# Scan stage of a Mamba-2 layer: operands loaded for four chunks at once, gates by chunk, output weights behind

## The reference

```python
def step(state, inp):
    x, dtq, bq, cq = inp
    cs = jnp.cumsum(dtq * a_g, axis=1)
    seg = cs[:, :, None] - cs[:, None, :]
    decay = jnp.exp(jnp.where(causal[None, :, :, None, None], seg, -jnp.inf))
    xdt = x * dtq[..., None]
    cb = jnp.einsum('bign,bjgn->bijg', cq, bq)
    y = jnp.einsum('bijgh,bjghp->bighp', cb[..., None] * decay, xdt)
    y = y + jnp.einsum('bign,bghpn->bighp', cq, state) * jnp.exp(cs)[..., None]
    to_end = jnp.exp(cs[:, -1:] - cs)
    state = state * jnp.exp(cs[:, -1])[..., None, None] + jnp.einsum(
        'bjgn,bjghp->bghpn', bq, to_end[..., None] * xdt)
    return state, y
# afterwards: y + d_skip * x, times silu(z), a grouped RMSNorm, the output projection
```

## Time and profile before

| | us |
|---|---|
| median of 3 runs (lowest to highest) | 3037.1 (3032.89 to 3038.3) |
| the profiled execution, its own time | 3036.6 |
| its span, first to last instruction | 3034.8 |
| TensorE / VectorE / ScalarE / GpSimd busy in the span | 2692.9 / 1908.8 / 1553.8 / 641.3 |
| scan stage, 1812 to 2117 us: TensorE / VectorE / ScalarE / GpSimd busy | 198.9 / 181.0 / 78.5 / 144.8 of 305 |
| mean granted TensorE clock in that stage, DMA share, GB/s | 0.80, 0.67, 165 |

### The profile page before, as it was taken

One profiled execution on the slowest core, in us unless ns is written; L12 is line 12 of the kernel. 1 busy time (PEld: TensorE's weight loads), 2 busy tenths in 40 slices (PEclk: granted clock), 3 DMA queues, 4 the chain that ended last, 5 costly groups with the idle time before them and its releaser, 6 DMA issues. The chain is left out here.

```text
span 3034.8 us, 40407 instructions
## 1 busy us (share of the span) xinstructions
PE 2692.9 (89%) x13762; PEld 2157.4 (71%) x13762; DVE 1908.8 (63%) x2393; ACT 1553.8 (51%) x1794; POOL 641.3 (21%) x530
## 2 busy tenths in 40 slices
PE   7998999987999999939999986676998799999992
PEld 6885677756887777828888864555787588888772
DVE  5335766337888888855235315665543688888885
ACT  4234555226888888744223212222122488888883
POOL 0000000003343343420000004544000134443340
PEclk9998999998999999959999997887999899999996
DMA  4325110146999999843223226665212599999995
GB/s 145 89 47 155 36 43 22 49 155 252 374 371 371 372 370 371 305 154 100 80 90 121 84 85 171 163 164 144 107 42 98 203 387 383 374 372 371 367 361 203
DMA packets 347895, 618.71 MB, mean 204 GB/s; under 512 B 33320, under 2 KB 135232, under 8 KB 347648
## 3 DMA queue, kind: packets, MB, share of 16 engines
q1 hardware_dynamic: 322880, 570.94, 55.3%
q0 software_dynamic: 19136, 33.61, 3.0%
q10 hardware_dynamic: 5760, 12.59, 1.1%
HBM read 566.55 MB, written 86.13 MB: 215 GB/s over the span
## 5 line engine op out<-in xcount | busy, mean ns | idle before, releaser
L2334 DVE TENSOR_TENSOR moe_w_low<-moes_raw,moe_w_high 128x2048 fp32r<-128x2048 f32 x384 | 868.5, 2289 | 163.3 <-ACT moe_w_high L2263 162.6
L2263 ACT ACTIVATE moe_w_high<-moes_raw 128x2048 fp32r<-128x2048 f32 x384 | 725.3, 1917 | 125.5 <-PEq L150 56.7
L2130 POOL COPY moe_pick<-moes_tokens 128x1 int32 (+1 forms) x64 | 88.6, 1384 | 595.2 <-PE moe_px L2179 594.5
L174 PE MATMUL moe_py<-moe_w_high,moe_h_high 128*128 128x512 f32 x512 | 209.1, 408 | 0.0
L174 PE MATMUL moe_pg<-moe_w_high,moe_x_high 128*128 128x512 f32 x512 | 205.1, 401 | 3.6 <-DVE moe_x_low L2384 3.6
L174 PE MATMUL moe_pu<-moe_w_high,moe_x_high 128*128 128x512 f32 x512 | 204.3, 399 | 0.0
L176 PE MATMUL moe_pg<-moe_w_high,moe_x_low 128*128 128x512 f32 x512 | 201.1, 393 | 0.0
L176 PE MATMUL moe_py<-moe_w_high,moe_h_low 128*128 128x512 f32 x512 | 201.0, 393 | 0.0
L176 PE MATMUL moe_pu<-moe_w_high,moe_x_low 128*128 128x512 f32 x512 | 200.6, 392 | 0.0
L175 PE MATMUL moe_pg<-moe_w_low,moe_x_high 128*128 128x512 f32 x512 | 200.0, 391 | 0.0
L175 PE MATMUL moe_py<-moe_w_low,moe_h_high 128*128 128x512 f32 x512 | 199.7, 390 | 0.0
(11 more groups left out here) (386 smaller groups left out, 6356.8 us busy)
## 6 DMA issues: line engine op xcount, KB each, us to landing
moes_raw<-in_w_gate SPq DMA_DIRECT2D x128, 1024.0 KB, 12.4
moes_raw<-in_w_up SPq DMA_DIRECT2D x128, 1024.0 KB, 12.6
moes_raw<-in_w_down SPq DMA_DIRECT2D x128, 1024.0 KB, 12.4
sproj_raw<-in_w_in_ssd SPq DMA_DIRECT2D x40, 512.0 KB, 4.2
comb_rows<-Y SPq DMA_DIRECT2D x32, 512.0 KB, 8.7
scan_sums<-CSR SPq DMA_DIRECT2D x32, 512.0 KB, 9.6
XC<-sproj_c SPq DMA_DIRECT2D x24, 512.0 KB, 5.0
HN<-plan_hn SPq DMA_DIRECT2D x16, 512.0 KB, 3.0
```

The costliest lines, as they stand in the source:

```text
L174: nc.tensor.matmul(out, lh, rh, start=start, stop=False)
L2130: nc.gpsimd.tensor_copy(pick[a][:, :], M.tokens[:, bass.ds(b, 1)]).then_inc(picked[a], 1)
L2263: nc.scalar.activation(wh[c % SPLIT_SLOTS][:, :], M.raw[j][:, :], ACT.Copy).then_inc(w_high, 1)
L2334: nc.vector.tensor_tensor(wl[j][:, :], M.raw[c % RAW_SLOTS][:, :], bits(wh[j][:, :]), ALU.subtract).then_inc(w_low, 1)
```

## The change

`LOAD = 4` chunks are loaded together. `bT`, `cT`, `xT` and `sums` get buffers four chunks wide, two of each instead of four narrow ones; `z` and `y` keep their ring of four. SyncE's new `operands(q)` loads quad q (half a group's chunks): two DMAs of 256 KB, one of 1024 KB and one of 2048 KB for sums. `gates(n)` loads z of one item. The semaphores are split: `loaded` (bT, cT, xT; TensorE waits for it), `sums_loaded` (VectorE) and `z_loaded` (GpSimd). From quad 2 on, `operands(q)` waits for `y_done` and, ahead of sums, for `seg_ok` of the last item of quad q - 2, but in SyncE's order it stands behind `gates(4q - 1)`, which waits until item 4q - 5 is gated. SyncE begins with quad 0, the z of items 0 to 3, quad 1, and then `early_dma`. No compute operation is added or removed; their operands are slices of the wide buffers.

```diff
--- before.py
+++ after.py
@@ -1384,13 +1384,13 @@
 
     GW, KT = HG * HD, HG * HD // P
     ITEMS = [(g, c) for g in range(G) for c in range(NT)]
-    NI, RING = len(ITEMS), 4
+    NI, RING, LOAD = len(ITEMS), 4, 4
     with Stage(nc, "scan") as st:
         PAR = range(2)
-        xT = [st.sb(f"xT{a}", [P, KT, P]) for a in range(RING)]
-        bT, cT = ([st.sb(f"{n}{a}", [P, P]) for a in range(RING)] for n in ("bT", "cT"))
+        xT = [st.sb(f"xT{a}", [P, KT, LOAD * P]) for a in PAR]
+        bT, cT = ([st.sb(f"{n}{a}", [P, LOAD * P]) for a in PAR] for n in ("bT", "cT"))
         z, y = ([st.sb(f"{n}{a}", [P, GW]) for a in range(RING)] for n in "zy")
-        sums = [st.sb(f"sums{a}", [P, HG, P]) for a in range(RING)]
+        sums = [st.sb(f"sums{a}", [P, HG, LOAD * P]) for a in PAR]
         cbm = [st.sb(f"cbm{a}", [P, P]) for a in PAR]
         dec, W = ([st.sb(f"{n}{a}", [P, HG, P]) for a in PAR] for n in ("dec", "W"))
         bt = [st.sb(f"bt{a}", [P, N]) for a in PAR]
@@ -1399,7 +1399,8 @@
         state = st.sb("state", [P, GW])
         pcb, pbt, pyi, pst = (st.ps(n, [P, HALF]) for n in ("pcb", "pbt", "pyi", "pst"))
         px, py = ([st.ps(f"{n}{a}", [P, GW]) for a in PAR] for n in ("px", "py"))
-        loaded, y_stored = ([st.sem(f"{n}{a}") for a in range(RING)] for n in ("loaded", "y_stored"))
+        z_loaded, y_stored = ([st.sem(f"{n}{a}") for a in range(RING)] for n in ("z_loaded", "y_stored"))
+        loaded, sums_loaded = ([st.sem(f"{n}{a}") for a in PAR] for n in ("loaded", "sums_loaded"))
         cb_done, x_turned, yi_done, st_done, y_done = (st.sem(n) for n in ("cb_done", "x_turned", "yi_done", "st_done", "y_done"))
         bt_ok, xs_ok, e_ok, ss_ok = (st.sem(n) for n in ("bt_ready", "xs_ready", "decay_ready", "squares"))
         cbm_ok, seg_ok, xdt_ok, yi_ok, y_ok, st_ok = (st.sem(n) for n in ("cbm_ready", "seg_ready", "xdt_ready", "yi_ready", "y_ready", "state_ready"))
@@ -1424,47 +1425,67 @@
         def byhead(x):
             return x.rearrange("p (h d) -> p h d", h=HG)
 
+        def chunk(n):
+
+            return n // LOAD % 2, slice(n % LOAD * P, (n % LOAD + 1) * P)
+
         def arrived(eng, n):
-            eng.wait_ge(loaded[n % RING], (n // RING + 1) * 80)
+            eng.wait_ge(loaded[n // LOAD % 2], (n // (2 * LOAD) + 1) * 48)
 
         @block.sync
         def _(sp):
-            early_dma(sp)
-            for n, (g, c) in enumerate(ITEMS):
-                a, tok = n % RING, slice(c * P, (c + 1) * P)
-                if n >= RING:
-                    sp.wait_ge(y_done, n - RING + 1)
-                    sp.wait_ge(gated, n - RING + 1)
-                    sp.wait_ge(seg_ok, n - RING + 1)
+            def operands(q):
+                (g, c), a = ITEMS[q * LOAD], q % 2
+                tok = slice(c * P, (c + LOAD) * P)
+                if q >= 2:
+                    sp.wait_ge(y_done, (q - 1) * LOAD)
                 for buf, first in ((bT, DI // P), (cT, DI // P + G)):
                     sp.dma_start(buf[a][:, :], K.XC[g + first, :, tok]).then_inc(loaded[a], 16)
                 sp.dma_start(xT[a][:, :, :], K.XC[g * KT:(g + 1) * KT, :, tok].rearrange("k p n -> p k n")).then_inc(loaded[a], 16)
-                sp.dma_start(sums[a][:, :, :], K.CSR[g * HG:(g + 1) * HG, tok].partition_broadcast(P)).then_inc(loaded[a], 16)
-                sp.dma_start(z[a][:, :], K.Z[tok, g * GW:(g + 1) * GW]).then_inc(loaded[a], 16)
+                if q >= 2:
+                    sp.wait_ge(seg_ok, (q - 1) * LOAD)
+                sp.dma_start(sums[a][:, :, :], K.CSR[g * HG:(g + 1) * HG, tok].partition_broadcast(P)).then_inc(sums_loaded[a], 16)
+
+            def gates(n):
+                (g, c), a = ITEMS[n], n % RING
+                if n >= RING:
+                    sp.wait_ge(gated, n - RING + 1)
+                sp.dma_start(z[a][:, :], K.Z[c * P:(c + 1) * P, g * GW:(g + 1) * GW]).then_inc(z_loaded[a], 16)
+
+            operands(0)
+            for n in range(RING):
+                gates(n)
+            operands(1)
+            early_dma(sp)
+            for n in range(RING, NI):
+                if n % LOAD == 0 and n >= 2 * LOAD:
+                    operands(n // LOAD)
+                gates(n)
 
         @block.tensor
         def _(pe):
             def front(n):
-                r = n % RING
+                r, tok = chunk(n)
                 arrived(pe, n)
                 if n:
                     pe.wait_ge(cbm_ok, n)
-                nc.tensor.matmul(pcb[:, 0:P], bT[r][:, :], cT[r][:, :], start=True, stop=True).then_inc(cb_done, 1)
+                nc.tensor.matmul(pcb[:, 0:P], bT[r][:, tok], cT[r][:, tok], start=True, stop=True).then_inc(cb_done, 1)
                 if n >= 2:
                     pe.wait_ge(xs_ok, n - 1)
                 if n:
                     pe.wait_ge(bt_ok, n)
                 for k in range(KT):
-                    nc.tensor.transpose(px[n % 2][:, k * P:(k + 1) * P], xT[r][:, k, :], K.ident)
-                nc.tensor.transpose(pbt[:, 0:P], bT[r][:, :], K.ident).then_inc(x_turned, 1)
+                    nc.tensor.transpose(px[n % 2][:, k * P:(k + 1) * P], xT[r][:, k, tok], K.ident)
+                nc.tensor.transpose(pbt[:, 0:P], bT[r][:, tok], K.ident).then_inc(x_turned, 1)
 
             def back(n):
-                (g, c), a, r = ITEMS[n], n % 2, n % RING
+                (g, c), a = ITEMS[n], n % 2
+                r, tok = chunk(n)
                 if c:
                     pe.wait_ge(st_ok, states(n - 1))
                     if from_state(n) > 1:
                         pe.wait_ge(yi_ok, from_state(n) - 1)
-                    nc.tensor.matmul(pyi[:, :], cT[r][:, :], state[:, :], start=True, stop=True).then_inc(yi_done, 1)
+                    nc.tensor.matmul(pyi[:, :], cT[r][:, tok], state[:, :], start=True, stop=True).then_inc(yi_done, 1)
                 if c + 1 < NT:
                     pe.wait_ge(bt_ok, n + 1)
                     pe.wait_ge(xde_ok, states(n))
@@ -1480,7 +1501,7 @@
                         pe.wait_ge(w_lo, n + 1)
                     if k == KT // 2:
                         pe.wait_ge(w_hi, n + 1)
-                    nc.tensor.matmul(py[a][:, k * P:(k + 1) * P], xT[r][:, k, :], skip[g % 2][:, k, :, :], start=True, stop=False)
+                    nc.tensor.matmul(py[a][:, k * P:(k + 1) * P], xT[r][:, k, tok], skip[g % 2][:, k, :, :], start=True, stop=False)
                     for h in (2 * k, 2 * k + 1):
                         last = nc.tensor.matmul(py[a][:, h * HD:(h + 1) * HD], W[a][:, h, :], xdt[a][:, h * HD:(h + 1) * HD],
                                                 start=False, stop=(h % 2 == 1))
@@ -1526,14 +1547,15 @@
             V = nc.vector
 
             def front(n):
-                (g, c), a, r = ITEMS[n], n % 2, n % RING
-                arrived(dve, n)
+                (g, c), a = ITEMS[n], n % 2
+                r, tok = chunk(n)
+                dve.wait_ge(sums_loaded[r], (n // (2 * LOAD) + 1) * 16)
                 if n >= 2:
                     dve.wait_ge(w_lo, n - 1)
                     dve.wait_ge(w_hi, n - 1)
                 for h in range(HG):
                     own = K.heads[:, CS, c, g * HG + h:g * HG + h + 1]
-                    last = V.tensor_scalar(dec[a][:, h, :], sums[r][:, h, :], own, 0.0, ALU.subtract, ALU.min)
+                    last = V.tensor_scalar(dec[a][:, h, :], sums[r][:, h, tok], own, 0.0, ALU.subtract, ALU.min)
                 last.then_inc(seg_ok, 1)
                 dve.wait_ge(cb_done, n + 1)
                 V.tensor_tensor(cbm[a][:, :], pcb[:, 0:P], K.upper, ALU.mult).then_inc(cbm_ok, 1)
@@ -1599,7 +1621,7 @@
             def gate(n):
                 a, r = n % 2, n % RING
                 pool.wait_ge(y_ok, n + 1)
-                arrived(pool, n)
+                pool.wait_ge(z_loaded[r], (n // RING + 1) * 16)
                 if n >= RING:
                     pool.wait_ge(y_stored[r], n // RING * 16)
                     pool.wait_ge(ss_ok, n - RING + 1)
```

## The result

The changed kernel takes 2982.8 us (median of four runs, 2980.02 to 2986.79) against 3037.7 us for the one before in the same comparison: a ratio of 0.982, with a 95% interval of 0.9804 to 0.984. That is 55 us less. The forecast was 2983.

What follows compares the result with a forecast made beforehand. It took VectorE's stalls on scan loads, mostly sums, as the bound. Loop saving 55.7 us plus 3.6 at the start minus 6 for late quads, 53.3 off 3036.6, gave 2983 us; range 2957 to 3033.

Steps and rivals of the forecast that it cites:

- What bounds the kernel before: Scan stage: VectorE loses 34 us in the loop to load stalls; sums is more than half of each load's time.
- (a): Scan loads: a quad's sums in 2 KB runs takes 10.5 us, interpolated towards the final gain's 4 KB row.
- (b): Scan start: with w_out moved behind the first loads, VectorE starts at 1829.5 instead of 1833.10, 3.6 us earlier.
- (c): Steady state of the scan loop: sums about half a microsecond late, charged 1 us on each of six quads, 6 us.
- A + 22.5: Time item 8's front wants its sums, counted from A, the start of item 3's y addition; sums predicted at A + 23.0.
- (d): Scan loop on VectorE: 31 periods of 7.1 us plus ends, 226.7 us against 282.4, saving 55.7 us.
- The cover: Scan loop: TensorE needs only 5.3 us an item at its upper clock level, which was expected to hold.
- Rival 1: Scan sums: repeated reads stay as slow per byte, 22 to 26 us a quad; 3061 to 3089 us, chance 0.11.
- Rival 2: Scan sums: no penalty at 2 KB, no late quads; 2972.5 us, or 2959 with periods of 6.66; chance 0.16.
- Rival 3: Scan loop: TensorE falls to 1.2 GHz in part, or its waits fill in; period 8.0 us, 3011 us, chance 0.18.
- Rival 4: Scan loop: stalls were only cover, VectorE's waits before y additions grow; 3031 to 3043 us, chance 0.05.
- The rule on 512 B: Scan sums: 512 B is the least transfer for line rate, so wider packets would bring sums nothing.

Runs made afterwards that it cites:

- e9: Changed kernel with bT, cT, xT and sums each loaded in four one-chunk DMAs of 512 B runs: 3035.0 us.
- e1: Changed kernel with the output weights (w_out, 4 MB) issued ahead of the first quad, as before: 2994.0 us.
- e3: Changed kernel with only bT, cT and xT in 512 B runs, sums staying in 2 KB runs: 2988.3 us.
- e11: Changed kernel with only sums in 512 B runs, read from eight different blocks with a row per partition, so decays are wrong: 3015.1 us.
- e2: Changed kernel with only sums in four DMAs of 512 B runs, the other operands staying in 2 KB runs: 3022.2 us.
- e12: Changed kernel with GpSimd's fade of the state cut from 512 to 64 columns, leaving seven of eight heads' states unfaded: 2966.2 us.
- e8: Changed kernel with scan_dec moved from VectorE to ScalarE, the sign turned round in the exponential: 2961.9 us.
- e10: e8 with GpSimd making xde ahead of its upper half of W: 2941.8 us.

## Why the prediction was right, point by point

The time was right, to less than a microsecond, and that closeness is luck. The mechanism was right, but its terms were not as good as the total: two were off by about 6 us each in opposite directions, and a third by 2.4.

- **What bounds the kernel before.** Right. The stalls came from the loads, sums took most of each load, and the wait's removal left VectorE as the bound. e9 shows that nothing is left of the gain without the long runs; e1, that some 11 of the 55 us need the output weights behind as well.
- **(a) Sums of a quad, 10.5 us.** Wrong in size: 6.2 us, 338 GB/s. The step that failed is the interpolation "three sevenths of the way" between 86 to 101 ns for a packet at 512 B and 262 ns at 4 KB. There is no such slope from 512 B on: a single load's packet has 88 to 102 ns at 512 B, 1 KB and 2 KB. The straight line put 161 to 170 ns where 97 were measured. At 2 KB this is near the rate of ordinary loads (370 GB/s, 89 ns a packet), so the bound from the full rate (5.7 us) was the one to take. Why the 4 KB row moved more slowly than that, at 205 to 300 GB/s, no run shows; it was a load of 512 KB, a quarter of the size. "The run length matters only for a repeated source" was right (e3 and e11).
- **(b) The start, 3.6 us earlier.** 6.0 were measured. 2.4 us more: sums landed 6.1 us behind xT instead of 11.1, and xT at 8.3 us after the stage's start (issued 0.8 in, landing 7.5 later) instead of 5.8. The 0.6 us for completion stands in no row.
- **(c) 6 us for late quads.** None came late: VectorE waits for sums once. With sums at 6.2 instead of 10.5 us a quad lands about 4 us before it is wanted, by the prediction's own account (A + 18.7 against A + 22.5). z for the gates and the queued 4 MB cost nothing, as said.
- **(d) The loop, 226.7 us.** 233.1 were measured. The cover held: the granted clock is 0.94 in the mean from 1824 to 2056 us (lower for short stretches, as 0.50 from 1874 to 1876, in which VectorE is busy throughout), and one y addition waits for scan_py. The mis-sized term is the period: 7.3, not 7.1. It was taken from dense items that came singly or in pairs, where the engines had just come out of a stall or went into one, and the longest was of two items. In an unbroken run two or more GpSimd operations stand beside nearly every group (26 of 30): 3.65 us in the mean, up to 5.07.
- **The sum.** The 4.3 us too much for sums made the 6 of (c), and in (b) with the late xT against it 2.4; (d) was 6.4 too little. The stage came out at 247.6 us against 16.9 + 232.7 = 249.6 predicted.
- **Rival 1** fell: a repeated read is not the same bytes per second at 2 KB. e9 and e2 show what it would have cost here: not 3061 to 3089, but 3022 to 3035. The stalls are 5 to 7 us, not 12 to 16, since four short-run loads in the queue take about 16 us and not 22 to 26. **Rival 2** had the packets right, and named 2972.5; it was off by the period. **Rival 3** fell by its cause (the clock is 1.00 from 1900 to 1932 us, 0.91 over the stage, and VectorE hardly waits), though its effect, a longer period, came in small and by way of GpSimd. **Rival 4** fell with the waits.
- **The rule on 512 B** (the Trainium skill, DMA: Bandwidth & Descriptors, section Specifications). By it e2 should have been as fast as the changed kernel. It is 39 us slower, and e11, with the same packets from a source that isn't repeated, has the changed kernel's loop. The measurement decides: here the rule holds for ordinary rows and not for rows that all partitions read.

## What to carry to other kernels

A load that spreads few rows over all partitions is worth longer runs: for the same 2.10 MB, 2 KB runs were some 2.6 times as fast here as 512 B runs. Runs beyond 2 KB were not tried. Ordinary loads can stay as they are. When stalls go, a period read from single dense items is a lower bound (7.1 against 7.3 here, and the longest stretch, of two items, would have given no more): count what the neighbouring engine will have beside them in an unbroken run. Where VectorE is the bound, an operation shortened on GpSimd can bring nearly as much (16.6 us, e12) as work taken from VectorE itself (21 us, e8); and once that is done, the order on GpSimd can be what TensorE waits for (20 us, e10).

## What the runs showed of the hardware

- A single load of 1024 packets from a source that all 128 partitions read takes 6.5, 5.6 and 6.2 us at 512 B, 1 KB and 2 KB a packet: 81, 187 and 338 GB/s. Four loads of 512 B packets queued together take 15.0 to 17.9 us (e2), 117 to 140 GB/s. The same 512 B packets from different rows moved at 291 to 302 GB/s (e11).
- A GpSimd operation of 1.04 to 1.3 us costs VectorE 0.8 to 1.0 us when it falls on scan_dec or scan_W, and is often longer itself, 1.50 or 1.64 instead of 1.04. Operations of VectorE that read PSUM are not touched.
- Cutting one such operation of GpSimd from 512 columns to 64 in 24 of 32 items brought 16.6 us of 2983 (e12).
